# Gate and up weights side by side, in one transfer, in a two-layer mixture-of-experts trunk

## The reference

```python
for l in range(DEPTH):                                   # DEPTH = 2
    h = _rms_norm(x, norm_mix[l])
    z = h @ w_in[l]                                      # 1024 x 3000
    ...                                                  # differential, sparse and latent attention
    x = x + jnp.concatenate([ya, yb, yc], -1) @ w_out[l] # 1024 x 1024
    x = x + _hier_moe(_rms_norm(x, norm_ffn[l]), ..., w_gate[l], w_up[l], w_down[l])

def expert_block(args):                                  # 32 experts per layer
    xb, e = args
    h = jax.nn.silu(xb @ w_gate[e]) * (xb @ w_up[e])     # both 1024 x 512
    return h @ w_down[e]                                 # 512 x 1024
```

## Time and profile before

| | |
|---|---|
| median of three runs | 1188.37 us (1188.06 to 1188.47) |
| span of the profiled execution | 1185.7 us, 2.7 us below the median of the runs |
| TensorE matmul / weight load / VectorE / ScalarE busy | 78% / 51% / 28% / 17% of the span |
| DMA: moved, mean rate | 447.80 MB, 378 GB/s |
| chain that ended last | DMA 60%, TensorE 35% |

### The profile page before, as it was taken

The page is one execution under the profiler, slowest core; times in us unless marked ns, Lnnn a source line. Parts: engine busy times, 40 slices in busy tenths (PEclk is TensorE's granted clock), DMA queues, the critical chain, the costliest instruction groups (busy, mean ns, idle before and its releaser), DMA issues.

```text
span 1185.7 us, 23487 instructions
## 1 busy us (share of the span) xinstructions
PE 921.0 (78%) x10312; PEld 605.4 (51%) x10317; DVE 333.8 (28%) x974; ACT 195.9 (17%) x529; POOL 18.4 (2%) x37
## 2 busy tenths in 40 slices
PE   9999999766676676766799999997585847566765
PEld 5876566444444343434478766665253525334532
DVE  3555652211111111111147465521111111111112
ACT  2244331010100010101022442211010101000102
POOL 1000000000000000000010001000000000000000
PEclk9999999987888789888999999999787978798888
DMA  8976499999999999999998156999999999999994
GB/s 304 389 299 236 194 366 428 428 423 429 424 429 423 428 425 426 426 427 425 403 388 324 46 226 269 378 425 426 427 424 428 426 425 427 425 427 425 425 428 206
DMA packets 60504, 447.80 MB, mean 378 GB/s; under 512 B 10832, under 2 KB 16368, under 8 KB 33264
## 3 DMA queue, kind: packets, MB, share of 16 engines
q1 hardware_dynamic: 57664, 443.49, 90.7%
q10 hardware_dynamic: 2736, 2.76, 0.7%
HBM read 442.57 MB, written 3.67 MB: 376 GB/s over the span
## 4 chain that ended last, share of the span: by engine, by line
DMA 60%; PE 35%; issue 1%; DVE 1%; SPq 1%; ACT 1%; POOL 0%; POOLq 0%; ACTq 0%; DVEq 0%
DMA ring<-in_w_up 41%; DMA arena<-in_w_up 11%; PE pv L1818 9%; PE pj L1439 8%; DMA arena<-in_w_down 8%; PE pj L1445 2%; PE pj L1545 2%; PE pj L1676 2%; PE pj L1651 1%; PE pj L1685 1%; PE tr L1840 1%; PE lg L1469 1%; SPq L593 1%; PE tr L1479 1%; PE pj L1850 1%
## 5 line engine op out<-in xcount | busy, mean ns | idle before, releaser
L1818 PE MATMUL pv<-ring,xT 128*32 128x256 f32 x3136 | 293.0, 454 | 145.8 <-DMA ring<-in_w_up 92.7
L1818 PEld LDWEIGHTS pv<-ring,xT 128*32 128x32 f32 x3136 | 147.4, 126 | 241.3 <-issue 191.9
L1284 DVE TENSOR_SCALAR arena<-arena 128x128 f32<-128x128 f32 x64 | 14.5, 227 | 678.7 <-ACT arena L860 678.4
L1818 PE MATMUL pv<-arena,xT 128*32 128x256 f32 x640 | 89.2, 436 | 28.7 <-DMA ring<-in_w_up 28.7
L675 ACT ACTIVATE arena<-pv 128x256 f32<-128x256 f32 x64 | 24.6, 384 | 525.8 <-PE pv L1818 525.8
L1439 PE MATMUL pj<-xT,ring 128*128 128x256 f32 x448 | 100.3, 381 | 0.0
L1840 PE MATMUL tr<-ring,arena 128*32 128x256 f32 x1376 | 83.0, 379 | 15.1 <-issue 15.1
L1439 PEld LDWEIGHTS pj<-xT,ring 128*128 128x128 f32 x448 | 84.1, 190 | 13.3 <-issue 1.2
L1850 PE MATMUL pj<-arena 32*128 32x256 f32 x512 | 72.5, 399 | 8.1 <-ACT arena L675 8.1
L1850 PE MATMUL lg<-arena 32*128 32x256 f32 x512 | 72.5, 400 | 0.0
L1818 PEld LDWEIGHTS pv<-arena,xT 128*32 128x32 f32 x640 | 46.1, 121 | 47.5 <-issue 39.6
(11 more groups left out here) (244 smaller groups left out, 950.7 us busy)
## 6 DMA issues: line engine op xcount, KB each, us to landing
ring<-in_w_gate SPq DMA_DIRECT2D x46, 2048.0 KB, 44.6
ring<-in_w_up SPq DMA_DIRECT2D x46, 2048.0 KB, 38.9
ring<-in_w_down SPq DMA_DIRECT2D x42, 2048.0 KB, 42.9
arena<-in_w_down SPq DMA_DIRECT2D x14, 2048.0 KB, 45.1
arena<-in_w_gate SPq DMA_DIRECT2D x12, 2048.0 KB, 44.8
ring<-in_w_in SPq DMA_DIRECT2D x10, 2048.0 KB, 21.2
arena<-in_w_up SPq DMA_DIRECT2D x8, 2048.0 KB, 39.3
ring<-in_w_out SPq DMA_DIRECT2D x4, 2048.0 KB, 21.3
```

Source lines behind the costliest of these rows:

```text
L1818: ins = mm(gu_ps[i * CAP:(i + 1) * CAP, :], xg[:, j, c:c + CAP], w, start=(j == 0), stop=(j == KD - 1), tile_position=(0, i * CAP), skip_g ...
```

## The change

The host program stores the weights in another layout before the launch: gate and up of an expert side by side (for each of a partition's eight rows first 512 gate values, then 512 up values, 32 KiB in one piece), each chunk of `w_in` and each half of `w_out` in one piece per partition. No arithmetic is done on them. In the kernel:

- the eleven places become four of 32 KiB per partition for gate and up together (`gu_place`: ring slots 0 and 1, 2 and 3, 4 and 5, and the two places of `arena`) and three of 16 KiB for down (`d_place`: ring slot 7, ring slot 6, and the one in `x` and `bias`);
- `x` and `bias` become one allocation `xb`, so that the last place is in one piece;
- gate and up of an expert come in one transfer of 4 MiB, to place `e % 4`; down comes in one of 2 MiB, to place `e % 3`. The planner goes. The order of issue is gate-up 0, gate-up 1, down 0, gate-up 2, down 1, ..., so down comes one expert later in the order than before;
- the transfers of the seam are written out (`first_experts`); they wait for the same events as before;
- the queue waits on semaphores by kind of place in place of one per slot.

```diff
-    start = (0, 1, 2, 3, 4, 5, 8, 9, 7, 6, 10)
...
-    frees = [by_name[n] for n in freed_in_order()]
...
-    for load, freed in zip(loads[ALL_SLOTS:], frees):
-        slot[load] = slot[freed]
...
+def loads_of(m):
+
+    order = [("gu", 0)]
+    for e in range(1, BODY - 1):
+        order += [("gu", e), ("d", e - 1)]
+    late = [("gu", BODY - 1), ("d", BODY - 2)] if m == ROUNDS - 1 else [("d", BODY - 2), ("gu", BODY - 1)]
+    return [(kind, m * BODY + e) for kind, e in order + late + [("d", BODY - 1)]]
...
-        x = sb("x", TOK * D_MODEL).rearrange("p (t f) -> p t f", t=TOK)
+        xb = sb("xb", TOK * D_MODEL + 9 * SEQ)
+        x = xb[:, 0:TOK * D_MODEL].rearrange("p (t f) -> p t f", t=TOK)
...
+        gu_place = [flat_ring[:, 2 * i * SLOT:2 * (i + 1) * SLOT].rearrange("p (j n) -> p j n", j=KD) for i in range(3)]
+        gu_place.append(late_place.rearrange("p (j n) -> p j n", j=KD))
+        d_place = [flat.rearrange("p (k n) -> p k n", k=KE) for flat in (ring[:, 7, :], ring[:, 6, :], xb[:, 0:SLOT])]
...
+                sp.wait_ge(steps_used, at(l, 2, 1))
+                sp.dma_start(gu_place[0][:, 0:2], again[:, 0:2]).then_inc(refill_in, 16)
+                sp.wait_ge(steps_used, at(l, 2, 2))
+                sp.dma_start(gu_place[0][:, 2:4], again[:, 2:4]).then_inc(refill_in, 16)
+                sp.wait_ge(gu_used[0], at(l, GU_FILLS, 1))
+                sp.dma_start(gu_place[0][:, 4:], again[:, 4:]).then_inc(gu_full[0], 16)
...
+                    for kind, e in loads_of(m):
+                        if kind == "gu" and e > REFILLED:
+                            i = e % GU_PLACES
+                            sp.wait_ge(gu_used[i], at(l, GU_FILLS, gu_uses(e)))
+                            sp.dma_start(gu_place[i], gu_v[l * N_EXPERTS + e]).then_inc(gu_full[i], 16)
+                        elif kind == "d" and e >= SPLIT:
+                            i = e % D_PLACES
+                            sp.wait_ge(d_used[i], at(l, D_FILLS[i], d_uses(e)))
...
+    steps = (a[n].reshape(DEPTH * N_EXPERTS, P, KD, D_EXPERT) for n in ("w_gate", "w_up"))
+    a["gate_up"] = np.concatenate(list(steps), 3).reshape(DEPTH * N_EXPERTS, P, 2 * SLOT)
```

More of the change, by code:

```diff
@@ L126, in bucket_one_hot @@
     return (np.arange(REL_BUCKETS)[:, None] == bucket[None, :]).astype(np.float32)
[L129 to L149, removed]
@@ new lines, with gu_uses, d_uses, gu_loads @@
+GU_PLACES, D_PLACES = 4, 3
+GU_LOADS = {1: 2, 2: 2}
+D_LOADS = {1: 2, 2: 2}
+SPLIT = GU_PLACES - 1
+REFILLED = GU_PLACES
+GU_FILLS = N_EXPERTS // GU_PLACES
+D_FILLS = [len(range(i, N_EXPERTS, D_PLACES)) for i in range(D_PLACES)]
+def gu_uses(e):
+    return sum(n % GU_PLACES == e % GU_PLACES for n in range(e))
+def d_uses(e):
+    return sum(n % D_PLACES == e % D_PLACES for n in range(e))
+def gu_loads(layer, e):
+    def upto(last):
+        return sum(GU_LOADS.get(n, 1) for n in range(last) if n % GU_PLACES == e % GU_PLACES)
+    return 16 * at(layer, upto(N_EXPERTS), upto(e + 1))
@@ L199, in at, with d_loads, upto @@
+def d_loads(layer, e):
+    def upto(last):
+        return sum(D_LOADS.get(n, 1) for n in range(last) if n % D_PLACES == e % D_PLACES)
+    return 16 * at(layer, upto(N_EXPERTS), upto(e + 1))
 def at(layer, per_layer, n):
@@ L374, in trunk @@
         lines = ring[:, 7, 1024:1024 + LINE]
[L377 to L378 removed]
+        win_full = [sem(f"win_full{i}") for i in range(len(WIN_CHUNKS))]
+        win_used = [sem(f"win_used{i}") for i in range(len(WIN_CHUNKS))]
+        wout_full, wout_used = ([sem(f"wout_{n}{i}") for i in range(2)] for n in ("full", "used"))
+        gu_full, gu_used = ([sem(f"gu_{n}{i}") for i in range(GU_PLACES)] for n in ("full", "used"))
+        d_full, d_used = ([sem(f"d_{n}{i}") for i in range(D_PLACES)] for n in ("full", "used"))
         gain_f_in = sem("gain_f_in")
@@ L435, in chunk, with win_v @@
             return ring[:, s, 0:KD * n].rearrange("p (j n) -> p j n", j=KD)
[L437 to L453, removed]
+        def win_v(l, i):
+            a, b = WIN_CHUNKS[i]
+            at_ = KD * sum(q - p for p, q in WIN_CHUNKS[:i])
+            return w_in_d[l][:, at_:at_ + KD * (b - a)].rearrange("p (j n) -> p j n", j=KD)
         def nk(t):
@@ L1675, in out_upper @@
                     for k in range(KD // 2, KD):
-                        mm(pj[:, half], mixT_up[:, t, k - KD // 2, :], weights(6 + half)[:, k, :], start=(k == KD // 2), stop=False)
+                        mm(pj[:, half], mixT_up[:, t, k - KD // 2, :], chunk(6 + half, 512)[:, k, :], start=(k == KD // 2), stop=False)
                 def out_lower(t, half):
@@ L1684, in out_lower @@
                     for k in range(KD // 2):
-                        ins = mm(pj[:, half], xT[:, k, t * P:(t + 1) * P], weights(6 + half)[:, k, :],
+                        ins = mm(pj[:, half], xT[:, k, t * P:(t + 1) * P], chunk(6 + half, 512)[:, k, :],
                                  start=False, stop=(k == KD // 2 - 1))
@@ L1809, in gather, with gate_up @@
                     return last
-                def gate_up(gate, up, c, other_half=0, signal=False):
+                def gate_up(both, c, other_half=0, signal=False):
                     for j in range(KD):
@@ L1938, in _ @@
                                 pe.wait_ge(over_full[0], i * 16 + 16)
-                                pe.wait_ge(over_full[1], i * 16 + 16)
-                                gate, up = (chunk(slot_of(l, c), 512) for c in range(2))
-                                gate_up([gate[:, j] for j in range(KD)], [up[:, j] for j in range(KD)], 0).then_inc(o_gu, 1)
+                                gate_up(gu_place[0], 0).then_inc(o_gu, 1)
                                 pe.wait_ge(o_gu_read, i + 1)
```

266 lines of the change are left out of this document (109 added, 157 removed).

## The result

Four runs of the changed kernel took 1193.45 to 1196.33 us, median 1195.30; the kernel before, on the same chip, 1188.21 (1187.81 to 1188.47). The ratio is 1.0059, with an interval of 1.0045 to 1.0073: slower by 7 us, where 9 us less was forecast. The profiled execution has a span of 1194.0 us, 8.3 more than before.

What follows compares the result with a forecast made beforehand. Bound: TensorE in attention, the never-empty DMA queue in the experts. 1185.7 - 7.4 (packets) - 3.0 (refill) + 0.8 (gap) = 1176.1 us span, plus 2.7 to the median: 1179 us; own range 1173 to 1186, 8-in-10 range up to 1187.

Steps and rivals of the forecast that it cites:

- Faster w_in and w_out: Attention weights of layer 1 arrive in some 39 us instead of 43 to 45; counted at nothing, in layer 0 the same.
- The two signs that the prediction named for being wrong: Prediction wrong if the expert stream's rate does not rise, or if TensorE waits in attention for `w_in`.
- the tail of 12.6 us: End of the kernel after the last expert: same order as before, so its 12.6 us do not change.
- one transfer later: Down comes one transfer later in the expert stream; TensorE's average wait of 4.3 us per awaited expert was set against it.
- Larger pieces in the stream: Expert weights: 32 KiB packets save packet prices on 54 pairs, 3.9 to 5.9 us; with split transfers, 7.4 us taken.
- The rival of two packets: Expert stream: 32 KiB go as two packets, giving 1184.7 us, between 1183 and 1188; chance 0.18.
- the split place: Expert stream: 14 transfers formerly sent in halves each lose 8 packets per engine, saving 1.0 to 1.5 us.
- The refill: Refill of expert 4 in larger pieces and three transfers: saves 1.5 us per layer, 3.0 us for two.
- The gap behind the refill: First transfer behind the refill waits for down 0, so engines run dry 0.4 us, 0.8 us for both layers.
- the fixed turns: Rival in the expert stream: places refilled in fixed turns leave the queue empty, slower or no gain, 1190 us; chance 0.07.
- the slower reading: Rival in the expert stream: partitions' shares 32 KiB apart are read more slowly, 1204 us at 411 GB/s; chance 0.07.
- The increments at the start: Eleven semaphore increments ahead of SyncE's first transfer go; counted at nothing.

Runs made afterwards that it cites:

- E3: Changed kernel with `w_in` in its old layout and down 29 sent ahead of gate-up 30; 1180.10 us, ratio 0.9929 to the kernel before.
- E4: Changed kernel with down 29 sent ahead of gate-up 30 and layer 0's `w_in` chunks 3 to 5 held until `bias_lines` landed; 1180.69 us.
- E1: Changed kernel with `w_in` alone back in its old layout; 1186.86 us, ratio 0.9989 to the kernel before.
- E5: Kernel before the change with only the new `w_in` layout; 1197.30 us, ratio 1.0071.
- E2: Changed kernel with down 29 sent ahead of gate-up 30 in the last round; 1189.24 us, ratio 1.0010 to the kernel before.
- E6: E4 with each gate-up transfer of the stream sent as two of 2 MiB, in 16 KiB packets; 1184.91 us.
- E8: E4 with gate and up apart in memory, still one 4 MiB transfer per pair but 16 KiB packets; 1185.33 us.
- E7: E4 with the eleven semaphore increments put back ahead of SyncE's first transfer; 1180.23 us.

## Why the prediction was wrong

1. *"Faster w_in and w_out ... I count this at nothing."* This step failed. It looked for who waits for `w_in` and for whether DMA has room, and found that neither matters; that holds, E3 and E4 are equal. It did not ask who else uses the DMA engines at that time. The rows were there: before, `bias_lines` landed at 22.94 + 14.1 = 37.0, and ScalarE came to the transfer that needs it at 38.32. That was a slack of only 1.3 us (in E4, where the table landed at 32.7, ScalarE issued it just as long after the first one, 15.4 us). And from 28 to 34 us the table's packets went one for one with SyncE's. With turns of 16 KiB the table had to be late. Price: 9.2 us by the table of stretches, 8.7 by the spans of E1, 8.9 by E5. The two signs that the prediction named for being wrong both stayed away: the stream's rate rose, and TensorE waited in no attention for `w_in`. The sentence of its forecast that was off is that both attentions take as long as before, to 0.5 us: the first took 9.2 us more.
2. *"... after the last expert the order is the same as before ..., so the tail of 12.6 us does not change."* The tail is 12.52 us, as said. But it had to be the turn of down 29 that was followed, one expert earlier, against TensorE's order: a 4 MiB transfer was put ahead of what TensorE needs first. Price: 6.1 us by E2, nearly the 4.1 + 2.2 us that the last downs start late. The sentence on down coming "one transfer later" took an average wait of 4.3 us as slack for all experts; this one waited 10.
3. *Larger pieces in the stream.* The mechanism held: 20198 packets for the forecast "about 20000", 429 GB/s in the range 428 to 430. The size was somewhat high. The 54 pairs were counted at 13.6 ns per packet, 5.9 of the 7.4 us; E6 and E8 give 4.2 to 5.1 us, between the two ends of 3.9 and 5.9. The choice of the upper end, for the sake of the slowest engine, was not borne out. The rival of two packets falls. E6 and E8 are its case with the two faults mended: they lie 3.5 and 3.1 us under the kernel before, where it had 3.7 for the split place, the refill and the gap.
4. *The refill.* 1.7 us in layer 0 by its landing, for 1.5. The mean of both layers by landings is 3.6 us for stream, refill and gap together, where the sum had (7.4 + 3.0 - 0.8) / 2 = 4.8.
5. *The gap behind the refill, the fixed turns, the slower reading.* With the two faults mended the span is 7.1 us under the one before, and the stretches from refill to last down are 422.7 and 421.6 us long (E3). There is no room for a hole of several us, and the stream moves 428 GB/s (250 to 580 us), so the rate is not slower.
6. *The increments at the start.* Nothing, as counted (E7).

The sum without the two faults would have been 1185.7 - 3.6 - 3.5 = 1178.6, which is the span of E3. So the terms that were worked out gave 7.1 of the 9.6 us that were forecast for them, and what was left out decided. The range was added up with a slip: packet terms of 10, a refill of 7.0 and no gap give 1171.4 as its lower end and not 1173, which changes nothing here. The Trainium skill ("DMA: Bandwidth & Descriptors", "Queues, rings and completion order") says that an engine goes round its queues packet by packet, and gives a packet several descriptors, 9 to 17 as a rule. The turns measured here are one contiguous piece each (15 of each queue in 0.6 us, 686 to 684 and 160 to 156 in 6 us), so the measurement decides. The rule of turns itself, which would have spoken against this change, was not weighed.

## What to carry to other kernels

In this kernel larger packets on one queue slowed the queue beside it, which got one packet for each of them. Before enlarging packets, list the transfers of the other queues in that stretch, with the slack of whoever waits for them, and either hold the large ones back or give the small ones larger pieces. When transfers are merged or reordered, set the order of issue against the order of use for every item near the end, where no later wait hides a late one. A term worked out well is no help if a step was set to nothing because one engine does not wait.

## What the hardware showed that was not expected

- The DMA engines alternated between two queues by one contiguous piece at each size tried: 686 to 684, 450 to 446, 273 to 275, 160 to 156 packets at 2, 4, 8 and 16 KiB.
- A contiguous piece of 32 KiB was one packet (6912 fewer packets than in E6), and a packet cost some 10 to 12 ns beside its bytes (E6, E8), much the same whether a transfer was split or only its memory was.
- Two pauses of TensorE were paid twice. Its granted clock stood at 0.50 (1.2 GHz) from 44 to 46 us, inside a wait of 7.6 us, and the 22 matmuls after it took 6.6 us instead of 4.1; after a wait of 9.95 us the next 32 took 3.64 instead of 1.93.
